# One-core, two-block kernel in 32-bit floats: part-wise operands at three norms, halves and quarters of the contraction in the first slots, the result stored in four pieces

## What is computed

```python
# first block, w_up is 2048 x 2*5504
x = x + gt1 * merge_groups(...)                      # output projection "mix_out"
h2 = rmsnorm(x, g_norm2) * (1 + sc2) + sh2           # norm "n2"
u = h2 @ w_up                                        # "up"
x = x + gt2 * ((silu(conv3x3(u_gate) + conv_b) * u_val) @ w_down)
# second block, i = 0 (pool mixer) and i = 1 (latent attention)
h = h + rms_norm(out, post_norm[i])                  # "post0", "post1"
gate = sigmoid(rms_norm(h, ple_norm[i]) @ ple_w_gate[i])   # "plegate0", "plegate1", 2048 x 2048
h = h + (p[i] @ ple_w_proj[i]) * gate                # "proj0", "proj1", 256 x 2048
```

## Time and profile before

| | |
|---|---|
| median of 3 runs | 2835.0 us (2826.0 to 2837.6) |
| profiled execution | 2836.5 us, span 2834.7 |
| busy TensorE, VectorE, ScalarE | 95%, 72%, 50% of the span |
| mean granted TensorE clock | 0.979 |
| longest chain | TensorE 66%, VectorE 7%, issue 3%, ScalarE 2% of the span |
| transfers | 530 MB, mean 187 GB/s |

### The profile page before, as it was taken

One profiled execution on the slowest core, in us unless ns is written; L12 is line 12 of the kernel. 1 busy time (PEld: TensorE's weight loads), 2 busy tenths in 40 slices (PEclk: granted clock), 3 DMA queues, 4 the chain that ended last, 5 costly groups with the idle time before them and its releaser, 6 DMA issues.

```text
span 2834.7 us, 42305 instructions
## 1 busy us (share of the span) xinstructions
PE 2700.3 (95%) x15974; PEld 2343.9 (83%) x15974; DVE 2027.8 (72%) x3081; ACT 1421.4 (50%) x2000; POOL 0.2 (0%) x4
## 2 busy tenths in 40 slices
PE   7899999999979999999999999999999899999988
PEld 3468778998868888888888888889988898988877
DVE  6676786985878888887556777776654888456576
ACT  6433433444445555554444665554444654665563
POOL 0000000000000000000000000000000000000000
PEclk9999999999989999999999999999999999999989
DMA  8667565640735545455555455544555445432433
GB/s 345 226 250 268 228 258 220 220 186 31 268 137 189 191 179 191 181 191 175 189 189 189 170 186 191 179 172 182 183 188 183 146 160 186 165 136 109 178 139 129
DMA packets 104534, 530.21 MB, mean 187 GB/s; under 512 B 8240, under 2 KB 8784, under 8 KB 51296
## 3 DMA queue, kind: packets, MB, share of 16 engines
q1 hardware_dynamic: 101888, 515.93, 49.8%
q10 hardware_dynamic: 2528, 12.66, 1.2%
HBM read 526.46 MB, written 2.10 MB: 186 GB/s over the span
## 4 chain that ended last, share of the span: by engine, by line
PE 66%; DVE 7%; issue 3%; ACT 2%; ACTq 0%; DVEq 0%; DMA 0%
PE ps L1973 33%; PE ps L1974 16%; PE ps L1965 4%; PE ps L1967 4%; PE ps L1966 4%; DVE lo L1096 2%; ACT hi L503 1%; PE ps L2310 1%; DVE ws L1691 1%; PE ps L2481 1%; PE ps L2479 0%; PE ps L2315 0%; ACT L866 0%; DVE R L1739 0%; DVE O L1737 0%
## 5 line engine op out<-in xcount | busy, mean ns | idle before, releaser
L1096 DVE TENSOR_TENSOR lo<-raw,hi 128x1024 fp32r<-128x1024 f32 x700 | 843.3, 1222 | 480.5 <-ACT hi L503 477.7
L503 ACT ACTIVATE hi<-raw 128x1024 fp32r<-128x1024 f32 x700 | 732.3, 1056 | 615.6 <-PE ps L1974 547.1
L1973 PE MATMUL ps<-x,hi 128*128 128x512 f32 x1376 | 487.6, 400 | 0.0
L1974 PE MATMUL ps<-x,lo 128*128 128x256 f32 x1376 | 387.0, 281 | 0.0
L1973 PE MATMUL ps<-y,hi 128*128 128x512 f32 x1024 | 364.2, 400 | 3.6 <-DVE y L1943 3.6
L1973 PE MATMUL ps<-xp,hi 128*128 128x512 f32 x1024 | 358.6, 396 | 5.5 <-DVE lo L1096 3.7
L1973 PEld LDWEIGHTS ps<-x,hi 128*128 128x128 f32 x1376 | 259.3, 188 | 64.8
L537 ACT ACTIVATE hi<-raw 128x1024 fp32r<-128x1024 f32 x162 | 167.3, 1054 | 275.7 <-PE ps L1967 115.4
L1974 PE MATMUL ps<-y,lo 128*128 128x256 f32 x1024 | 288.9, 282 | 0.0
L1974 PE MATMUL ps<-xp,lo 128*128 128x256 f32 x1024 | 284.7, 278 | 0.0
L1167 DVE TENSOR_TENSOR lo<-raw,hi 128x1024 fp32r<-128x1024 f32 x162 | 192.5, 1220 | 104.8 <-ACT hi L537 104.7
(11 more groups left out here) (385 smaller groups left out, 5015.3 us busy)
## 6 DMA issues: line engine op xcount, KB each, us to landing
raw<-in_weights SPq DMA_DIRECT2D x483, 1024.0 KB, 4.8
wlast<-in_weights ACTq DMA_DIRECT2D x8, 1024.0 KB, 4.8
xf<-in_xt SPq DMA_DIRECT2D x8, 512.0 KB, 9.5
raw<-in_weights SPq DMA_DIRECT2D x4, 768.0 KB, 4.3
R<-in_xt ACTq DMA_DIRECT2D x1, 2048.0 KB, 7.3
out<-R SPq DMA_DIRECT2D x1, 2048.0 KB, 6.3
maskn<-in_maskn ACTq DMA_DIRECT2D x1, 512.0 KB, 3.4
ptr<-in_pt ACTq DMA_DIRECT2D x2, 256.0 KB, 3.8
```

What stands on the lines that cost most here:

```text
L503: act.activation(HI[p % PAIR][:, c], RAW[p % RING][:, c], ACT.Copy).then_inc(hi_ready, 1)
L1096: dve.tensor_tensor(LO[p % PAIR][:, c], RAW[p % RING][:, c], HI[p % PAIR][:, c].bitcast(F32), ALU.subtract).then_inc(lo_ready, 1)
L1973: pe.matmul(o, h, pair[:, :, k, :], start=start, stop=False, **kw)
L1974: return pe.matmul(o[:, 0, :], l, pair[:, 0, k, :], start=False, stop=stop, **kw)
```

## The change

The column sums of the last two groups of w_mod follow one another without VectorE between them, and VectorE adds their biases once both are there. FINAL_TURNS is one turn earlier throughout, and the second half of the slot that turn 15 splits is split later, amid the operand. The operands of n2, ple0 and ple1 are made in five parts of 2, 2, 4, 4 and 4 blocks (PLE_PARTS). The first two slots of `up` hold one half each of the contraction of both first output blocks (`first_up`); the first four slots of each gate hold one quarter each of the contraction of the first four outputs, which gather in four banks of PSUM. Their loads pick the same bytes in another order. In `after_block` ScalarE's root stands ahead of the copy of the projection, the copy of its second half and the squares move behind the operand, and slots 1 to 3 of the gate are split between the parts. Outputs 0 to 7 of a gate are taken two in a turn, in turns 4 to 7; the sum of squares enters after the fourth slot. The result is stored in four pieces.

```diff
-FINAL_TURNS = (3, 5, 6, 8, 9, 11, 12, 14)
+FINAL_TURNS = (2, 4, 5, 7, 8, 10, 11, 13)
...
+PLE_PARTS = [(0, 2), (2, 2), (4, 4), (8, 4), (12, 4)]
+STORES = [(0, 8), (8, 4), (12, 2), (14, 2)]
+GATE_TURNS = {u: (2 * u - 8, 2 * u - 7) for u in range(4, 8)}
...
+        def gate_bank(u, r):
+
+            return (5, 6, 7, 2)[u] if isinstance(u, int) and u < 4 else (0, 1, 3, 4)[r]
...
+                elif kind == "up" and k < 2:
+                    w = place("up", 0)
+                    words = words.rearrange("p (a c) -> p a c", c=1024)
+                    stored = A["weights"][w:w + 2, :, 1024 * k:1024 * (k + 1)].rearrange("a p c -> p a c")
+                elif kind in ("plegate0", "plegate1") and k < 4:
+                    w = place(kind, 0)
+                    words = words.rearrange("p (a c) -> p a c", c=512)
+                    stored = A["weights"][w:w + 4, :, 512 * k:512 * (k + 1)].rearrange("a p c -> p a c")
...
-            sp.wait_ge(sem("gate1_used"), 1 + KD)
-            sp.dma_start(out, R[:, :]).then_inc(sem("stored"), 16)
-            sp.wait_ge(sem("stored"), 16)
+            for first, count in STORES:
+                sp.wait_ge(sem("gate1_used"), 1 + first + count)
+                sp.dma_start(out[:, first * T:(first + count) * T], blk(R, first, count)).then_inc(sem("stored"), 16)
+            sp.wait_ge(sem("stored"), 16 * len(STORES))
...
-                split("mix_out", u // RING, u % RING)
+                split("mix_out", u // RING, u % RING, 2, range(1 if u == 15 else 2))
...
             root("n2", rs[:, :], PS[2][:, 0:T], D)
-            for q in range(4):
+            split("mix_out", 3, 3, 2, range(1, 2))
+            for q, (first, count) in enumerate(PLE_PARTS):
                 act.wait_ge(sem("operand_made"), reached("made", "n2", q + 1))
-                for b in range(4 * q, 4 * q + 4):
+                for b in range(first, first + count):
                     ins = act.activation(blk(x2h, b), blk(tn, b), ACT.Identity, bias=mods[:, 96 + 2 * b:97 + 2 * b])
...
-                    act.wait_ge(halves_used, 2 * (where("up", i, r) + 1))
+                    act.wait_ge(halves_used, 2 * (where("up", i, r) + (2 if first else 1)) - (1 if first else 0))
...
+
+                def gained(i):
+                    act.wait_ge(sem("part_ready"), reached("part", name, i + 1))
+                    first, count = PLE_PARTS[i]
+                    for b in range(first, first + count):
+                        ins = act.activation(blk(hi, b), blk(R, b), ACT.Copy, scale=v(name, b))
+                    ins.then_inc(sem("operand_hi"), 1)
+
+                def square(q):
+                    act.activation(blk(squares, 4 * q, 4), blk(R, 4 * q, 4), ACT.Square).then_inc(sem("squares_ready"), 1)
+
+                split(f"proj{tag}", 0, 0)
                 root(f"post{tag}", rs[:, :], PS[2][:, 0:T], D)
-                proj(tag, pj, 1)
-                square(f"ple{tag}", squares, R, f"ple{tag}", hi)
+                proj_out(tag, pj, 0)
+                gained(0)
+                gained(1)
+                split(f"proj{tag}", 0, 1)
+                gained(2)
+                square(0)
+                split(f"plegate{tag}", 0, 0)
+                gained(3)
+                square(1)
+                split(f"plegate{tag}", 0, 1)
+                gained(4)
+                proj_out(tag, pj, 1)
+                square(2)
+                square(3)
 
             def gate(tag, tail=0):
...
-                        gated_hi(u - 1)
+                    if not isinstance(u, int) or u >= 2:
+                        split(name, i, r)
+                    if isinstance(u, int) and u == 3:
+                        gate_right(0, 0)
+                        gate_right(1, 1)
+                        root(f"ple{tag}", rs[:, :], PS[4][:, 0:T], D)
+                        gate_sigmoid(0, 0)
+                    for o, x in [(o, o % 4) for o in GATE_TURNS.get(u, ())] if isinstance(u, int) and u < 8 else [(u, r)]:
+                        if not isinstance(o, int) or o >= 2:
+                            gate_right(o, x)
+                        if not isinstance(o, int) or o:
+                            gate_sigmoid(o, x)
...
-                dve.wait_ge(sem("sums_taken"), g + 1)
+                dve.wait_ge(sem("sums_taken"), max(g + 1, 16) if g >= 14 else g + 1)
...
             n2_sum(15)
             recip("n2", rs[:, :])
             dve.wait_ge(sem("n2_gained"), 16)
-            for q in range(5):
-                if q < 4:
-                    t = by_head(blk(tn, 4 * q, 4))
-                    dve.tensor_tensor(t, t, rs[:, None, :].to_broadcast([P, 4, T]), ALU.mult).then_inc(sem("operand_made"), 1)
+            for q in range(6):
+                if q < 5:
+                    first, count = PLE_PARTS[q]
+                    t = by_head(blk(tn, first, count))
+                    dve.tensor_tensor(t, t, rs[:, None, :].to_broadcast([P, count, T]), ALU.mult).then_inc(sem("operand_made"), 1)
                 if q:
                     dve.wait_ge(sem("operand_hi"), reached("hi", "n2", q))
-                    for b in range(4 * q - 4, 4 * q):
+                    first, count = PLE_PARTS[q - 1]
+                    for b in range(first, first + count):
                         ins = dve.scalar_tensor_tensor(blk(x2l, b), blk(tn, b), mview[:, 48 + b, 0:1], blk(x2h, b).bitcast(F32),
                                                        ALU.add, ALU.subtract)
                     ins.then_inc(sem("operand_rest"), 1)
+                if q == 2:
+                    split("mix_out", 3, 3, 2, range(1, 2))
...
-                for q in range(5):
-                    if q < 4:
-                        g = by_head(blk(O, 4 * q, 4))
-                        own.done(dve.tensor_tensor(g, g, rs[:, None, :].to_broadcast([P, 4, T]), ALU.mult))
-                        own.wait()
-                        dve.tensor_tensor(blk(R, 4 * q, 4), blk(R, 4 * q, 4), blk(O, 4 * q, 4), ALU.add).then_inc(sem("part_ready"), 1)
-                    if q:
-                        gained_rest(f"ple{tag}", q - 1, R, f"ple{tag}", xh_, xl_)
-                    if q == 3:
-                        split(f"proj{tag}", 0, 1)
+                normed(0)
+                normed(1)
+                part_rest(0)
+                part_rest(1)
+                normed(2)
+                split(f"proj{tag}", 0, 1)
+                part_rest(2)
+                normed(3)
+                split(f"plegate{tag}", 0, 0)
+                part_rest(3)
+                normed(4)
+                split(f"plegate{tag}", 0, 1)
+                part_rest(4)
...
-                pe.wait_ge(sem("mods_ready"), 4 + g)
+                pe.wait_ge(sem("mods_ready"), 4 + min(g, 14))
...
                 out_major("mix_out", i, r, yh, yl, "y", halves_of(y, KD))
+            def first_up(s):
+
+                slot = BASE["up"] + s
+                p = slot % PAIR
+                pe.wait_ge(lo_ready, 2 * slot + 2)
+                for n in range(BLOCKS):
+                    a, k = n % 2, n // 2
+                    for part, (first, _) in enumerate(PLE_PARTS):
+                        if a == 0 and first == 8 * s + k:
+                            pe.wait_ge(sem("operand_rest"), reached("x", "n2", part + 1))
+                    c = slice((8 * a + k) * P, (8 * a + k + 1) * P)
+                    ins = mm2(a, HI[p][:, c], LO[p][:, c], halves_of(x2, KD), 8 * s + k, s + k == 0, s == 1 and k == 7)
+                    if n >= BLOCKS - 2:
+                        ins.then_inc(halves_used, 1)
+
             sum_squares("n2", "steps")
...
                     pe.wait_ge(sem("ff_made" if r % 2 else "pad_made"), 2 * i + (r // 2 - 1))
-                out_block("up", i, r, x2h, x2l, r, "n2", halves_of(x2, KD))
+                if isinstance(i, int) and i == 0 and r < 2:
+                    first_up(r)
+                else:
+                    out_block("up", i, r, x2h, x2l, r, None, halves_of(x2, KD))
             for s in range(4 * DOWN_SLOTS):
...
             def gate(tag, gh, gl, tail=0, pair=None):
+
+                name, ple = f"plegate{tag}", f"ple{tag}"
+                pe.wait_ge(evacuated, EVAC[f"proj{tag}"] + 1)
+                for q in range(4):
+                    def product(n, h, l):
+                        o, k = gate_bank(n // 4, 0), 4 * q + n % 4
+                        if n == 0 or q + k == 2:
+                            pe.wait_ge(sem("operand_rest"), reached("x", ple, q + 2 if q or n else 1))
+                        if pair is not None:
+                            return mm2(o, h, l, pair, k, k == 0, k == 15)
+                        return mm3(PS[o][:, 0:T], h, l, blk(gh, k), blk(gl, k), k == 0, k == 15)
+                    slot(name, 0, q, product)
                 pe.wait_ge(evacuated, EVAC[f"proj{tag}"] + 2)
-                for i, r in turns(pe, 16, tail, lead=1):
+                sum_squares(ple, "ssq", PS[4][:, 0:T])
```

(13 more changed lines are left out.)

103 lines of the change are left out of this document (46 added, 57 removed).

## The result

| | before | after |
|---|---|---|
| median | 2835.5 us (4 runs, 2826.0 to 2837.6) | 2794.2 us (4 runs, 2788.3 to 2803.4) |
| ratio, 95% interval | | 0.987 (0.984 to 0.9905) |
| profiled execution, span | 2836.5, 2834.7 | 2803.4, 2801.6 |

The changed kernel is 41.3 us faster by the medians and 33.1 by the two profiled executions; 2798.2 had been predicted. Six more executions gave 2802.2, a ratio of 0.988 (0.986 to 0.990).

A forecast was written before the change was run, and what follows sets the result against it. TensorE was taken to bound the kernel, fully busy in the feed-forward, with idle time to remove at four places. 12.9 + 8.8 + 11.3 + 3.8 = 36.8 us off the median 2835.0 gave 2798.2; range 2788 to 2811.

The forecast's parts named there:

- Place 1: From the last output projection into the feed-forward: TensorE ends the second slot of `up` 12.9 us earlier.
- R: VectorE's last addition to R before the feed-forward comes at 798.2 instead of 801.27, 3.1 us earlier.
- The root: At both gates, ScalarE's root ahead of its copy of the projection: the reciprocal starts 2.0 us earlier.
- S: Time of a gate's first matmul, moved from 2219.16 to 2214.0 and from 2726.24 to 2721.1.
- The single waits: TensorE's waits ahead of a gate's slots two to four: about 1.3, 0.6 and 0.6 us.
- The lag behind the pairs: First gate, outputs taken two in a turn: VectorE late for slot 10, 1.3 us lost, 8.8 kept.
- nothing is lost: Last gate: a pair of outputs makes a VectorE turn of 5.7 us, so pairing costs no time.
- place 3: Start of the last gate: fourth slot and norm sum done at 2747.1 instead of 2758.4, 11.3 us gained.
- Rival 2: VectorE's lag in the first gate passes into the next projection: 8.8 us lost, gain 28, 2807; chance 0.09.
- Store: End of the kernel: the last 256 KB land in 2.5 us, gaining 3.8 us, between 2.5 and 4.0.
- rival 1: Clock low through both gates' first two slots and longer entering the feed-forward: gain 22.8 us, 2812; chance 0.10.
- The absolute marks: Predicted times in the new trace of the two gates' first matmuls, near 2201 and 2699.

The follow-up runs named there:

- warm: Changed kernel plus ten matmuls that nobody reads in TensorE's idle time between mix_out and up; 2804.3 us, executed once.
- gate_whole: Changed kernel with whole output blocks instead of contraction quarters in the first four slots of both gates; 2817.3 us, executed once.

## Why the prediction was right, and where it was not

- **Place 1** (12.9 predicted, 13.15 measured). R: 3.1 and 3.1. From the end of mix_out to `up` 8.15 and 7.74, since the norm's sum, which I had at its old length, ran at full clock (0.70 us instead of 1.22); the two slots 14.3 and 14.27. The half clock over the first 5.2 us of `up` was in the sum, and warm shows that it costs nothing there. Slot three was ready in time: slots three and four take 5.65 each.
- **Gates.** The root 2.0 each, measured 1.9 and 1.9. First matmul earlier by 5.2 and 5.1 against the projection's start, measured 4.84 and 4.87. Fourth slot done at S + 25.8 and the norm's sum behind it; the next slot starts at S + 25.89 and S + 25.78. The single waits in the last gate were 1.12, 0.35 and 0.36 against 1.3, 0.6 and 0.6, the slots longer by what that leaves.
- **The lag behind the pairs.** First gate: 1.3 predicted; behind the fourth slot it takes 70.59 us against 69.28, 1.3, of which 1.1 lies around the wait ahead of slot 10 and 0.2 in slot 4 behind the norm's sum, which stood further ahead before. Last gate: "nothing is lost" was the step that failed: 1.0 us (67.76 against 66.72) was lost, 0.85 of it around that wait and 0.2 in slot 4. I gave a paired turn 5.7 us. It takes 6.8:

```profile
2747.51 2.36 DVE L1130 TENSOR_TENSOR lo<-raw,hi 128x1024 fp32r<-128x1024 f32 x2 [0.64 <-ACT hi L521]
...
2751.96 0.42 DVE L1820 TENSOR_TENSOR sgt<-sgt,ps 128x256 f32<-128x256 f32 x1 [0.51 <-ACT sgt L952]
...
2754.28 2.36 DVE L1130 TENSOR_TENSOR lo<-raw,hi 128x1024 fp32r<-128x1024 f32 x2 [0.64 <-ACT hi L521]
```

  I added VectorE's instructions and left out the two waits for ScalarE in a turn, 0.64 and 0.51, the same omission as in gate_whole's expectation. So place 3 is 10.2 instead of 11.3. Rival 2, that the lag does not heal, is out: behind slot 10 no wait is left.
- **Store.** 3.8 predicted, 4.25 measured; 256 KB land in 2.0 us, not 2.5.
- **Clock.** 0.94 and 1.00 in the gates' starts: rival 1 is out. The Trainium skill ("TensorE: Matmul & The Clock Gate", section "HAM oscillation — how this bites in real kernels") describes a kernel in which bursts of matmuls alternate with waits of 3 to 5 us and whose clock falls back to half in every round. Had the gates' starts gone that way, rival 1's price for them, 12 us, would have left 24.8 of the 36.8 us. The traces do not show it for the changed kernel, whose pauses there are 1.9 us and shorter, and agree for gate_whole, whose pauses are 2.9 to 4.6: 0.60.
- **The absolute marks** (gates near 2201 and 2699, measured 2202.7 and 2702.7) and the profiled time (2799.7, measured 2803.4) came out late by what I did not know of, the pace, though the front part was 3.65 us early. I took 5.65 us a slot for a constant of the machine. The range held 2794.2, as its width rested on a spread of 11.6 us between three executions whose cause I had not looked for. How near the median came is in part luck: two of its four executions took 2788 us and two 2800 and 2803, and six more had a median of 2802.2.

## What to carry to other kernels

Look for what a long wait really hangs on: here an instruction of 0.15 us that stood behind a whole operand was worth 11 us beside the other edits, and they brought 2.1 us without its removal. When a turn of one engine is priced, its waits for the other engine inside the turn belong to the price; where work is moved into those gaps, it costs nothing there. A stretch at half clock is worth repairing only where TensorE, not the engine that feeds it, is the slower one. Where TensorE is, as in the old start of the first gate, the same code took 1.5 us longer in one trace than in another. And where executions of a kernel differ by more than the change at hand, compare lengths between two instructions of the traces, and count matmuls in a stretch in which TensorE never pauses.
